# A first unit of the Up stage computed from rows without the norm's factor, and the sums of squares of that norm put between its rows

## What is computed

```
x = x + rmsnorm(merged @ w_o, g_mix_post)
h2 = rmsnorm(x, g_ffn_pre)
up, gt = jnp.split(h2 @ w_ffn_up, 2, axis=-1)
uc, new_ffn = causal_dwconv(up, prev_ffn, ffn_conv_w)
f = (jax.nn.gelu(uc + ffn_conv_b, approximate=True) * gt) @ w_ffn_down
x = x + rmsnorm(f, g_ffn_post)
x = x + jax.nn.sigmoid(x @ w_ple_gate) * (p @ w_ple)
```

## Time and profile before

| | us |
|---|---|
| median of 3 runs | 2731.82 (2731.69 to 2732.69) |
| time of the profiled execution | 2733.41 |
| its span, first to last instruction | 2731.4 |
| TensorE matmul busy in the span | 2707.9 (99%) |
| DVE busy | 2212.4 (81%) |
| ACT busy | 1332.5 (49%) |
| POOL busy | 30.3 (1%) |
| mean granted TensorE clock | 0.998 of full |

### The profile page before, as it was taken

The page is one execution under the profiler, slowest core; times in us unless marked ns, Lnnn a source line. Parts: engine busy times, 40 slices in busy tenths (PEclk is TensorE's granted clock), DMA queues, the critical chain, the costliest instruction groups (busy, mean ns, idle before and its releaser), DMA issues.

```text
span 2731.4 us, 54671 instructions
## 1 busy us (share of the span) xinstructions
PE 2707.9 (99%) x20915; PEld 2625.8 (96%) x20915; DVE 2212.4 (81%) x3890; ACT 1332.5 (49%) x2405; POOL 30.3 (1%) x52
## 2 busy tenths in 40 slices
PE   9999999999999999999999999999999999999999
PEld 8999999999999999889999999999998999989899
DVE  5988888777754578888888888888887778889898
ACT  5444455555542245545555555555553452435344
POOL 0000000000000000000000000000000000000000
PEclk9999999999999999999999999999999999999999
DMA  6333333333453323533333233233334243233553
GB/s 223 118 117 117 117 119 115 119 124 121 146 189 137 130 93 101 210 135 128 115 107 136 104 119 124 104 137 106 111 132 160 100 155 109 99 123 121 192 209 117
DMA packets 117792, 357.83 MB, mean 131 GB/s; under 512 B 13145, under 2 KB 35297, under 8 KB 115024
## 3 DMA queue, kind: packets, MB, share of 16 engines
q1 hardware_dynamic: 115440, 350.04, 36.2%
q0 software_dynamic: 2048, 5.68, 0.9%
q10 hardware_dynamic: 144, 0.15, 0.0%
HBM read 311.74 MB, written 45.32 MB: 131 GB/s over the span
## 4 chain that ended last, share of the span: by engine, by line
PE 96%; DVE 2%; issue 1%; ACT 0%; DMA 0%; SPq 0%; DVEq 0%; ACTq 0%
PE pair L977 73%; PE pair L943 8%; PE pair L1050 7%; PE pair L912 3%; PE pair L749 1%; PE pair L1020 1%; PE pair L817 1%; PE pair L840 1%; PE pair L1073 1%; PE pair L831 1%; DVE v_lo L1769 0%; PE pair L765 0%; DVE lo L1872 0%; DMA s_raw<-in_sstream 0%; DVE nv_s L1556 0%
## 5 line engine op out<-in xcount | busy, mean ns | idle before, releaser
L977 PE MATMUL pair<-o_hi,v_hi 128*128 128x260 f32 x5628 | 1597.0, 284 | 3.3 <-DVE v_lo L1769 2.7
L977 PE MATMUL pair<-o_hi,v_lo 128*128 128x260 f32 x5628 | 1588.9, 282 | 0.0
L1135 ACT ACTIVATE v_hi<-s_raw 128x512 fp32r<-128x512 f32 (+1 forms) x1296 | 807.3, 626 | 1001.8 <-PE pair L977 808.3
L977 PE MATMUL pair<-lo,v_hi 128*128 128x260 f32 x4020 | 1136.1, 283 | 0.0
L1769 DVE TENSOR_TENSOR v_lo<-s_raw,v_hi 128x512 fp32r<-128x512 f32 (+1 forms) x1232 | 837.5, 681 | 293.9 <-ACT v_hi L1135 247.9
L977 PEld LDWEIGHTS pair<-o_hi,v_hi 128*128 128x128 f32 x5628 | 1058.1, 188 | 17.5 <-issue 13.0
L977 PEld LDWEIGHTS pair<-o_hi,v_lo 128*128 128x128 f32 x5628 | 1060.2, 188 | 0.0
L977 PEld LDWEIGHTS pair<-lo,v_hi 128*128 128x128 f32 x4020 | 755.5, 188 | 0.3
L977 PE MATMUL pair<-lo_E,v_hi 128*128 128x260 f32 x804 | 227.5, 283 | 0.0
L977 PE MATMUL pair<-lo_A,v_hi 128*128 128x260 f32 x804 | 226.7, 282 | 0.0
L1135 ACT ACTIVATE v_hi<-s_one 128x512 fp32r<-128x512 f32 (+1 forms) x204 | 127.4, 626 | 155.3 <-PE pair L977 148.5
(11 more groups left out here) (216 smaller groups left out, 2306.4 us busy)
## 6 DMA issues: line engine op xcount, KB each, us to landing
s_raw<-in_sstream SPq DMA_DIRECT2D x468, 512.0 KB, 4.9
s_raw<-in_sstream SPq DMA_DIRECT2D x32, 384.0 KB, 3.7
f_scr<-fo SPq DMA_DIRECT2D x88, 130.0 KB, 1.9
g_scr<-d_h SPq DMA_DIRECT2D x16, 520.0 KB, 2.7
g_in<-g_scr SPq DMA_DIRECT2D x32, 260.0 KB, 2.7
x_scr<-y_sb SPq DMA_DIRECT2D x8, 1040.0 KB, 4.5
raw<-f_scr SPq DMA_DIRECT2D x7, 1040.0 KB, 4.9
raw<-in_x SPq DMA_DIRECT2D x4, 1040.0 KB, 6.6
```

Of the source, the lines that this page charges most:

```text
L977: mm = pe.matmul(out, wt[:, slot, kk * P:kk * P + P], r[:, k, :], start=j in (0, 1, 3) and k == 0 and n == 0, stop=k == nk - 1 and n == 2, ...
L1135: nc.scalar.activation(v_hi[:, n % 4, 0:width], src, ACT.Copy, scale=0.5 if u == "br" else 1.0).then_inc(v_hi_rdy, 1)
```

## The change

The first Up unit takes x times the norm's weight, without the factor; ACT makes those rows (`raw_row`) right behind each row's square. The tiles of `p @ w_ple` and the sums of squares are ordered anew: 11 tiles ahead of the first sum, sums 0 to 7 between and behind tiles 11 to 15, sums 8 to 15 between rows 1 to 5 of the plain unit. The factor is then multiplied into the same rows in place (`h2_row`, behind TensorE's reading of them) for all other units, eight rows ahead of t1, eight ahead of t2; and into the first unit's results, the up half in `fzb` (ahead of the convolution) and the gelu's output (which stands in for the gate half's factor). A POOL fill of `sq_acc`, which lies in the same memory as `rstd`, waits for the last use of the factor.

```diff
+            X_SUMS = {1: (8,), 2: (9, 10), 3: (11, 12), 4: (13, 14), 5: (15,)}
+            def x_sum(n):
+                if n == 0:
+                    pe.wait_ge(inv_ready, 2)
+                pe.wait_ge(xsq_ready, n + 1)
+                for h in range(2):
+                    mm = pe.matmul(pair[2][:, h, 0:HALF], ones[:, :],
+                                   sq_x[n % 4][:, h * HALF:(h + 1) * HALF],
+                                   start=n == 0, stop=n == KD - 1, skip_group_check=True)
+                mm.then_inc(xsq_summed if n < KD - 1 else sum_ready, 1)
...
             def plain_unit(s, also={}):
...
-                    pe.wait_ge((h_rdy, None, h2_rdy, None, None, None, xn_rdy)[s],
+                    pe.wait_ge((h_rdy, None, u_rdy, None, None, None, xn_rdy)[s],
                                (KD if s == S_GATE else 0) + k + 1)
...
+                    for n in also.get(k, ()):
+                        x_sum(n)
...
-            for t in range(2, 9):
+            for t in range(2, KD):
                 ple_tile(t)
+                for n in {10: (0,), 11: (1, 2), 12: (3,), 13: (4, 5), 14: (6,), 15: (7,)}.get(t, ()):
+                    x_sum(n)
...
+            def raw_row(n):
+                nc.scalar.activation(x_tile(n), two(y_sb[:, n, :]), ACT.Copy,
+                                     scale=chan[:, C_FFNPRE + n:C_FFNPRE + n + 1]).then_inc(u_rdy, 1)
...
             for n in range(KD):
                 square_x(n)
-                if n in (5, 9, 13):
-                    ple_evac(9 + (n - 5) // 4)
+                raw_row(n)
+                if n in (1, 2, 3, 5, 6, 7, 8):
+                    ple_evac((9, 10, 11, None, 12, 13, 14, 15)[n - 1])
...
+            def h2_row(k):
+                rows_done(U_UP, k)
+                dve.tensor_tensor(x_tile(k), x_tile(k), two(rstd[:, :]), ALU.mult).then_inc(h2_rdy, 1)
...
+                if s == 2:
+                    for k in range(KH):
+                        h2_row(k)
+                    dve.wait_ge(h2_rdy, KH)
+                    both_halves(t1, s)
                 both_halves(s1, u + 1)
                 both_halves(s3, u + 1)
-                both_halves(t1, s)
+                if s == 2:
+                    for k in range(KH, KD):
+                        h2_row(k)
+                    dve.wait_ge(h2_rdy, KD)
+                else:
+                    both_halves(t1, s)
                 both_halves(t2, s)
...
+                if t == 0:
+                    st.done(dve.tensor_tensor(ge[:, :], ge[:, :], rstd[:, :], ALU.mult))
+                    st.wait()
...
+                if t == 1 and i == 5:
+                    first = fzb[0][:, 2:2 + T]
+                    dve.wait_ge(c11_out, U_UP + 1)
+                    dve.wait_ge(c12_out, U_UP + 1)
+                    dve.tensor_tensor(first, first, rstd[:, :], ALU.mult).then_inc(z_scaled, 1)
```

More of the change, by code:

```diff
@@ L451, in build @@
         x_stored = [sem(f"x_stored{i}") for i in range(4)]
+        u_rdy = sem("u_rdy")
         h2_rdy = sem("h2_rdy")
+        z_scaled = sem("z_scaled")
         p_split_hi = sem("p_split_hi")
@@ L892, in banks_free, with plain_unit @@
                     pe.wait_ge(c11_out if j == 0 else c22_out, u)
-            def plain_unit(s):
+            X_SUMS = {1: (8,), 2: (9, 10), 3: (11, 12), 4: (13, 14), 5: (15,)}
[8 more added lines that the diff above has]
+                mm.then_inc(xsq_summed if n < KD - 1 else sum_ready, 1)
+            def plain_unit(s, also={}):
                 u, _, nk = SETS[s]
@@ L949, in first_unit @@
                 if SETS[s][0] in PLAIN:
-                    plain_unit(s)
+                    plain_unit(s, X_SUMS if s == 2 else {})
                     return
@@ L1429, in _ @@
                 square_x(n)
-                if n in (5, 9, 13):
-                    ple_evac(9 + (n - 5) // 4)
-            ple_evac(12)
-            ple_evac(13)
+                raw_row(n)
+                if n in (1, 2, 3, 5, 6, 7, 8):
+                    ple_evac((9, 10, 11, None, 12, 13, 14, 15)[n - 1])
             root(2)
-            ple_evac(14)
-            ple_evac(15)
             warm(ACT.Gelu_apprx_tanh, 3)
@@ L1451, in tap @@
                 act.wait_ge(c12_out, u + 1)
+                if t == 0:
+                    act.wait_ge(z_scaled, 1)
                 nc.scalar.activation(fcv[:, 0:TP], fzb[t % 2][:, 0:TP], ACT.Copy,
@@ L1474, in _ @@
             act.wait_ge(x_stored[3], 16)
-            act.wait_ge(h2_rdy, KD)
             plain_unit(2, fzb[0][:, 2:2 + HALF], fzb[0][:, 2 + HALF:2 + T], g_half[0][:, :], None)
@@ L2185, in _ @@
             dve.wait_ge(rstd_ready, 2)
-            new_x(C_MIXPOST, 0, {3: lambda: v_low(PLE_S + 6), 10: lambda: v_low(PLE_S + 7)})
+            new_x(C_MIXPOST, 0, {3: lambda: v_low(PLE_S + 6), 7: lambda: v_low(PLE_S + 7)})
             invert(2)
             dve.wait_ge(rstd_ready, 3)
[L2190 to L2198, removed]
             def conv(t, step):
@@ L2207, in conv @@
                 if step == 0:
+                    if t == 0:
+                        dve.wait_ge(z_scaled, 1)
                     dve.wait_ge(c11_out, U_UP + t + 1)
@@ L2348, in _ @@
                                a_st[n % 2][:, :, :]).then_inc(a_stored[n % 2], 16)
-            pool.wait_ge(h2_rdy, KD)
+            pool.wait_ge(u_rdy, KD)
             for c in (2, 3):
@@ L2354, in _ @@
                 pool.memset(z[:, 0:2], 0.0).then_inc(pool_set, 1)
+            pool.wait_ge(f_ready, 1)
             pool.memset(sq_acc[:, :, :], 0.0).then_inc(sq_h_added, 1)
```

## The result

The changed kernel takes **2739.91 us** (median of 8 runs, 2737.16 to 2740.65), the kernel before beside it 2731.99 (8 runs, 2731.04 to 2733.01): ratio 1.0028, 95% interval 1.0019 to 1.0037, slower by 7.9 us. The profiled execution took 2739.88, its span 2737.9 against 2731.4, mean clock 0.996 against 0.998. The forecast of 2737.5 is 2.4 us low; the time lies in the range of 2734.0 to 2741.0 and on the side forecast.

What follows compares the result with a forecast made beforehand. TensorE, busy 2707.9 of 2731.4 us, was taken as the bound. Second unit's later start 3.2, clock 1.75 and multiplication 0.76 sum to +5.7 us; against the median, 2737.5 us, range 2734.0 to 2741.0.

Steps and rivals of the forecast that it cites:

- What it gives: Around the Up stage: without the early hole and waits, TensorE finishes the plain unit at 1185.6, 6.1 us earlier.
- The second unit's start: Second Up unit: the late factor delays its start to 1195.45, 3.2 us later, leaving a 9.9 us hole.
- the named wait: Ahead of the second Up unit: TensorE's wait on c11_out, ACT's copy of the plain results, forecast to start at 1195.0.
- The clock after the hole: Second Up unit's first product: lower clock after the long idle time costs 1.75 us, ends 0.9 and 2.3.
- the 2.3 that the prediction hung on this: Upper end for the clock after the hole, taken if a restart begins at 1.2 GHz; total would be 0.55 higher.
- The prediction's lower end: Clock after the hole: 0.9 us, half of 1.75, as part of the low stretch may lie inside the hole.
- The two multiplications: On DVE: the one on fzb[0] costs nothing; the one on ge lies on the path in full, 0.76 us.
- Everything behind the third unit only shifts: After the third Up unit: no further cost; the sum stays +5.7 us.
- the conversion to the median: Profiled forecast 2739.1 lowered to 2737.5, because before's profiled execution lies 1.6 us above its median of 2731.82.
- Hole without clock: Rival: same hole ahead of second unit, but clock costs nothing or multiplications hide; +3.2 to +4.9 us, chance 0.14.
- Not held: Rival: copy comes before 1185.6, second unit starts at 1186.1, no clock lost; -5.4 us, 2726.4, chance 0.05.
- The longer chain: Rival: ACT and last sum late, or clock takes 2.3 and fill disturbs; +6.5 to +9.5 us, chance 0.17.

Runs made afterwards that it cites:

- copies run: Changed kernel with ACT's copies of the first Up unit's results put ahead of high parts 2 to 4: 2731.65 us, ratio 0.9998.
- sums: Changed kernel with sums 7 and 8 ahead of the plain unit and sums 9 to 15 behind its rows 0 to 3: 2737.82 us, ratio 1.0020.
- work in the hole: Changed kernel with 20 fp32 matmuls of ones, 8.9 us, between the plain and the second unit: 2736.03 us, ratio 1.0015.
- edits to the kernel before: Kernel before with activations' low parts 5 and 6 made later, 2730.26 us; or with only one weights' low part put ahead of part 5, 2731.35 us.
- gelu: Changed kernel without the multiplication of the gelu's output by the factor: 2736.58 us, ratio 1.0019.
- all mended: Changed kernel with copies ahead of part 2, sums earlier, part 4 moved into second unit, one low part ahead of part 5, t2 to t4 by halves: 2728.58 us.
- POOL on the changed kernel: Changed kernel with the multiplication on the gelu's output done by POOL instead of DVE: 2740.20 us, ratio 1.0031.
- low parts made late: Activations' low parts 5 and 6 made later: on the changed kernel 2736.07 us, on the kernel before 2730.26, with everything else mended 2727.63.

## Why the prediction was right, and where not

The profile of after is 0.41 us ahead of that of before when the tiles come (the last pair of tile 8 starts at 1132.21, not 1132.62), so 0.41 is added below.

- **What it gives.** Forecast: the plain unit at 1150.41, last sum done 1168.0, end 1185.6. Found: 1149.91, 1167.5 (1167.12 is the next row's start), 1185.2. Right; ACT kept up.
- **The second unit's start.** Forecast 1195.45, +3.2. Found 1195.01, +2.8; the 0.4 less is the 0.5 by which the last sum came earlier. The copies run, which moves three instructions on ACT and wins 8.3 us, shows that the named wait is the cause.
- **The clock after the hole.** Forecast 1.75, found 5.41 against 3.59 from product to product, 1.82; filling the hole gives the same 1.82. The chip was at the lower level, 1.2 GHz, before TensorE began again: the window up to 1194.60 has 0.67, that behind it 0.50. The Trainium skill ("TensorE: Matmul & The Clock Gate", "What's actually happening") calls the throttled clock the default state, which activity releases. The trace agrees in that the first matmul behind the hole ran at the lower level; the 2.3 that the prediction hung on this was not found here. The prediction's lower end went by the thought that part of the low stretch may lie inside the hole: part of it does, but by the two windows (0.67 over 9.78 us, 0.50 over 3.70) the stretch is some 10.2 us long, against 3.4 behind the short holes, so what was left behind the hole still cost as much. Over the runs profiled with this hole the first product took 5.25 to 6.47, 1.5 to 2.7 more than 3.75, so 2.7 had been the better upper end.
- **The two multiplications.** That on `fzb` cost nothing: the idle time of 0.73 behind it shrank to 0.11. With that on `ge` the matmul of the third unit that waits for the low part starts 5.45 later than before; less 2.77 and 1.82 that leaves 0.86 for a forecast of 0.76. The wait is 1.81 for a forecast of 1.9. The fill of `sq_acc`, for which a possible 0.2 was named, cost nothing either: it took 0.53 from 1221.42, and `lo_A` of DVE beside it took 2.38, as before.
- **The step that failed** is "Everything behind the third unit only shifts". The prediction lengthened a wait from 1.16 to 1.9 us and counted only the wait. Behind it the clock fell for 3.4 us, about 1.6 us more. The trace of before had the like in front of the reader: a hole of 1.83 us with a low stretch of 3.55 behind it. The size is that of this profile; in sums and in the work in the hole the same stretch cost 1.3 and 1.4, and in two of five profiles it did not come.
- **A second slip is in the conversion to the median.** The profiled execution of before lay 1.6 above its median, and the prediction took 1.6 off the changed kernel as well; there the profiled execution (2739.88) is the median (2739.91). From profile to profile the sum said +5.7 and +6.5 was found: 2.77 + 1.82 + 0.86 + 1.6, less the 0.41 ahead of it all and about 0.1. Before's profile holds two events that its other executions need not have: the low clock behind the first hole, which costs 1.1 (the five sums, merged in one row, take 6.31; 5.23 in both profiles of edits to the kernel before, behind the same 1.83 us of idle time and at full clock), and that at the gate, 1.7. The first goes away with the change and is already in its gain; taken off again with the median it counts twice. That it is the one which before's median run lacks was not tested.
- **The rivals.** Hole without clock: out, by the work in the hole. Not held: out as it stands, yet it is what one edit on ACT gives; its -5.4 became no difference to before, since it had not counted the 4.2 us of waits for ACT and DVE that follow. The longer chain: the measured time lies in its 2738.3 to 2741.3 and not in the forecast's own 2736.7 to 2738.3, but none of its mechanisms (late squares, a slow last sum, 2.3 for the clock, a fill that disturbs) was there. The total range held because it took this rival in, not because the forecast had seen the 1.6.

## What to carry over

Work taken out of a producer's way and put behind it must be followed to every instruction queued in front of the one that the bottleneck engine waits for; here a copy that needed nothing from the moved work stood behind work that did. Where an edit makes a wait of the matmul engine longer, price the clock behind it too (here 1.3 to 1.6 us, in three of five profiles). A profiled execution that lies off the median may carry such an event; find out which, and whether the change removes it, before shifting a forecast by the difference.

## What was not expected of the hardware

**The same hole does not always cost the clock.** The gate's second unit follows 2.45 to 2.47 us of idle time in all 13 profiles. In seven (before, after, copies, sums, gelu, all mended, POOL on the changed kernel) its first product takes 5.21 to 5.43, in six 3.74 or 3.75, as here with the low parts made late:

```profile
2581.26 3.74 PE L960 MATMUL pair<-y_sb,s_raw 128*128 128x260 f32 x16 [2.46 <-issue]
```

The first sum of squares of the kernel before waits 1.83 us in three profiles (before, and the two edits to it); behind it the clock fell in one. Behind the third unit's wait of 1.79 to 1.81 the clock fell in three profiles (changed, sums, work in the hole) and stayed in two (copies, POOL); behind 0.93 to 1.57 it fell in none of five. So one kernel's times come in groups some 1.5 to 2 us apart: of the 27 runs of before beside the last kernels five lie at 2729.6 to 2730.0 and none from there to 2730.8, most near 2731.5 and six at 2732.8 to 2733.4. That each group is a count of low stretches is seen in the profiled executions; for the others it is an inference from their times. What decides in a given run whether a wait is followed by one stays open.

**POOL's multiplication** of two 128x520 fp32 tiles took 4.13 and 4.14 us, six times DVE's 0.69, and did not lengthen DVE's instructions beside it (2.38 for two of `lo`, as elsewhere). How long it takes with DVE idle was not measured, so part of it may be waiting for DVE.
